# A two-layer hybrid decoder on one core: second layer's weights split in the first layer's pair stage, feed-forward operand without its norm, output projection in two half-K parts

## What is computed

```python
for l in range(DEPTH):
    h = rms_norm(x, norm_gains[l, 0])
    z = h @ w_in[l]
    z_main, z_mem = z[..., :MAIN_W], z[..., MAIN_W:]
    if l < N_A_LAYERS:
        y_main = pool_mixer(z_main, w_pool[l], pool_scale[l])
    else:
        y_main = dilated_mixer(z_main, positions, shared)
    y_mem = memory_attn(z_mem, mem, mem_norm[l], w_mkv[l])
    y = jnp.concatenate([y_main, y_mem], axis=-1) @ w_out[l]
    x = x + rms_norm(y, norm_gains[l, 1])
    h = rms_norm(x, norm_gains[l, 2])
    gu = h @ w_gate_up[l]
    y = (jax.nn.silu(gu[..., :D_FF]) * gu[..., D_FF:]) @ w_down[l]
    x = x + rms_norm(y, norm_gains[l, 3])
    if l == N_A_LAYERS - 1:
        shared = build_shared_kv(x, positions, kv_norm, w_kv)
```

## Time and profile before

| | |
|---|---|
| median of the runs | 2314.24 us (2311.76 to 2314.56) |
| profiled execution | 2309.91 us, of it the span 2308.0 us |
| TensorE busy | 2150.7 us, 93% |
| VectorE busy | 1337.2 us, 58% |
| ScalarE busy | 880.6 us, 38% |
| GpSimd busy | 264.9 us, 11% |
| HBM traffic | 170.04 MB read, 43.12 MB written |
| mean granted TensorE clock | 0.972 of full |

### The profile page before, as it was taken

How to read it: one execution, slowest core, us unless ns; L and a number is a source line. 1 busy time by engine, 2 the same in 40 slices (tenths; PEclk the granted TensorE clock), 3 DMA queues, 4 the chain that set the end, 5 groups by cost and what they waited for, 6 DMA issues and landing times.

```text
span 2308.0 us, 24943 instructions
## 1 busy us (share of the span) xinstructions
PE 2150.7 (93%) x9554; PEld 1719.2 (74%) x9554; DVE 1337.2 (58%) x1984; ACT 880.6 (38%) x1375; POOL 264.9 (11%) x136
## 2 busy tenths in 40 slices
PE   5997999999999999987999999895999999999996
PEld 4775877888888887875777767673788888888785
DVE  7355287566666626456445446469846666662543
ACT  5335343222223425232545556564422222242420
POOL 4442100000000000043122215120000000000000
PEclk9998999999999999998999999997999999999998
DMA  4202051222223536450000000014222222262533
GB/s 155 89 14 94 25 177 50 82 83 82 82 82 120 200 129 211 129 203 18 19 28 28 28 25 12 24 47 146 83 78 82 82 82 82 101 222 90 208 122 107
DMA packets 69382, 214.77 MB, mean 93 GB/s; under 512 B 7825, under 2 KB 10129, under 8 KB 64017
## 3 DMA queue, kind: packets, MB, share of 16 engines
q1 hardware_dynamic: 53136, 183.82, 23.1%
q10 hardware_dynamic: 16128, 29.37, 3.8%
HBM read 170.04 MB, written 43.12 MB: 92 GB/s over the span
## 4 chain that ended last, share of the span: by engine, by line
PE 79%; DVE 12%; issue 3%; ACT 3%; DMA 2%; POOL 0%; ACTq 0%; SPq 0%; DVEq 0%
PE PS L772 10%; PE PS L773 10%; PE PS L774 10%; PE PS L589 8%; PE PS L590 7%; PE PS L592 7%; PE PS L792 7%; PE PS L794 6%; PE PS L793 6%; PE PSC L697 4%; PE PO L671 2%; DVE SS L1436 2%; DVE RSTD L1428 1%; PE PTR L681 1%; DVE PR L1539 1%
## 5 line engine op out<-in xcount | busy, mean ns | idle before, releaser
L792 PE MATMUL PS<-IH,DH 128*128 128x512 f32 x704 | 275.7, 392 | 3.3 <-DVE IL L1744 2.9
L794 PE MATMUL PS<-IH,DL 128*128 128x512 f32 x704 | 274.0, 389 | 0.0
L793 PE MATMUL PS<-IL,DH 128*128 128x512 f32 x704 | 274.0, 389 | 0.0
L772 PE MATMUL PS<-BHT,SH 128*128 128x512 f32 x576 | 224.1, 389 | 0.0
L773 PE MATMUL PS<-BLT,SH 128*128 128x512 f32 x576 | 224.1, 389 | 0.0
L774 PE MATMUL PS<-BHT,SL 128*128 128x512 f32 x576 | 224.1, 389 | 0.0
L589 PE MATMUL PS<-XH,WH 128*128 128x512 f32 x448 | 196.0, 437 | 26.7 <-DVE XL L1566 21.2
L590 PE MATMUL PS<-XL,WH 128*128 128x512 f32 x448 | 180.7, 403 | 0.0
L2073 POOL TENSOR_TENSOR WR<-WR,GN 128x1024 f32<-128x1024 f32 x28 | 59.8, 2140 | 1003.8 <-DMA WR<-in_w 983.6
L2079 POOL TENSOR_TENSOR WL<-WR,WH 128x1024 fp32r<-128x1024 f32 (+2 forms) x66 | 145.3, 2203 | 217.0 <-ACT WH L899 217.0
L772 PE MATMUL PS<-BH,SH 128*128 128x512 f32 x432 | 168.0, 389 | 0.0
(11 more groups left out here) (205 smaller groups left out, 4327.8 us busy)
## 6 DMA issues: line engine op xcount, KB each, us to landing
DR<-in_wdn SPq DMA_DIRECT2D x64, 704.0 KB, 4.1
SR<-in_wst SPq DMA_DIRECT2D x36, 1024.0 KB, 5.2
WR<-in_w SPq DMA_DIRECT2D x60, 512.0 KB, 3.5
IR<-inner SPq DMA_DIRECT2D x88, 256.0 KB, 5.7
inner<-TP SPq DMA_DIRECT2D x36, 512.0 KB, 4.4
TP<-x_mid ACTq DMA_DIRECT2D x48, 256.0 KB, 3.0
x_mid<-YOA ACTq DMA_DIRECT2D x32, 256.0 KB, 2.7
XS<-in_x SPq DMA_DIRECT2D x16, 256.0 KB, 6.3
```

Of the source, the lines that this page charges most:

```text
L772: MM(BANK[bank], SH[b][:, w, c], BH[t][:, k, :], start=(k == 0), stop=False)
L792: MM(bank, wh[:, i, :], IH[r][:, :], start=(k == 0), stop=False)
L793: MM(bank, wh[:, i, :], IL[r][:, :], start=False, stop=False)
L794: ins = MM(bank, wl[:, i, :], IH[r][:, :], start=False, stop=(k == NF - 1))
```

## The change

It has five parts.

**1. Layer 1's weights for "mem", "in" and "kv" (24 blocks, `PRE`) are split during layer 0's pairs.** In sixteen pairs (f = 4 to 19), one and two weights in turn, SyncE loads a weight, ScalarE applies the gain in eight 128-wide copies and makes hi in one 1024-wide copy, GpSimd makes lo, and SyncE stores both to a buffer in HBM. In layer 1 both parts are loaded in place of the raw weight, and neither ScalarE nor GpSimd has work with them.

```diff
+def presplit(o):
+    return o.l == 1 and o.name in ("mem", "in", "kv")
...
+PRE = [n for n, o in enumerate(JOBS) if o.share is None and presplit(o)]
+PRE_AT = {n: i for i, n in enumerate(PRE)}
+NV = 3
+PRE_PAIRS = 16
+def prepared(f):
+    a, b = (len(PRE) * min(max(g - NHT, 0), PRE_PAIRS) // PRE_PAIRS for g in (f, f + 1))
+    return range(a, b)
...
+            def keep_weight(i):
+                b, o = i % NV, JOBS[PRE[i]]
+                act.wait_ge(v_loaded[b], 16 * (i // NV + 1))
+                for k in range(KT):
+                    ins = A(VR[b][:, k, :], VR[b][:, k, :], ACT.Copy, scale=GN[:, 8 * o.gain + k:8 * o.gain + k + 1])
+                    ins.then_inc(v_gained, 1)
+                act.wait_ge(v_gained, KT * (i + 1))
+                A(VH[b][:, :, :], VR[b][:, :, :], ACT.Copy).then_inc(v_hi, 1)
...
-                    silu_first(q)
+                    if l == 0:
+                        silu_first(q)
+                        for i in prepared(f):
+                            keep_weight(i)
                     if f < NF - 1:
...
+            for i in range(len(PRE)):
+                pool.wait_ge(v_hi, i + 1)
+                G_.tensor_tensor(VL[i % NV][:, :, :], VR[i % NV][:, :, :], as_f32(VH[i % NV][:, :, :]),
+                                 ALU.subtract).then_inc(v_lo, 1)
...
+                        for i in prepared(f - 2):
+                            keep_weight(i)
+                        for i in prepared(f):
+                            load_kept(i)
```

```diff
-                pe.wait_ge(ss_done[h], 8 * (s + 1))
-                px_begin(("norm", s, h))
-                MM(PX[:, :], ONES, SS[:, HALF[h]], start=True, stop=True).then_inc(px_full, 1)
-
...
+            def norm_columns(s, h):
+                if s:
+                    pe.wait_ge(ss_done[h], 8 * s)
+                else:
+                    pe.wait_ge(ss0_done, 8)
+                px_begin(("col", s, h))
+                for t in range(4):
+                    c = HT * h + P * t
+                    ins = MM(PX[:, t:t + 1], SS[:, c:c + P], ONE, start=True, stop=True)
+                ins.then_inc(px_full, 1)
+            def norm_rows(s, h):
+                rows.append((s, h))
+                pe.wait_ge(rc_done, len(rows))
+                px_begin(("row", s, h))
+                for t in range(4):
+                    ins = nc.tensor.transpose(PX[:, P * t:P * (t + 1)],
+                                              RC[:, 4 * h + t:4 * h + t + 1].to_broadcast([P, P]), IDENT)
+                ins.then_inc(px_full, 1)
...
+            def norm_row(s, h):
+                px_read(("row", s, h), lambda: A(RSTD[:, HALF[h]], PX[:, :], ACT.Copy))
...
-            def norm(s, h):
-
-                dve.wait_ge(px_free, px_at[("norm", s, h)])
-                V.reciprocal(RSTD[:, HALF[h]], RSTD[:, HALF[h]]).then_inc(rstd_done[h], 1)
+            def invert(s, h):
+                dve.wait_ge(px_free, px_at[("col", s, h)])
+                V.reciprocal(RC[:, 4 * h:4 * h + 4], RC[:, 4 * h:4 * h + 4]).then_inc(rc_done, 1)
```

```diff
+                if r == 3:
+                    A(bh(h, k), YO[h][:, k, :], ACT.Copy, scale=GN[:, 48 + k:49 + k]).then_inc(x_hi[h], 1)
...
+            def scale_x(h, k):
+                act.wait_ge(x_lo[h], 16 + k + 1)
+                act.wait_ge(*x_stored(3, h, k))
+                A(YO[h][:, k, :], YO[h][:, k, :], ACT.Copy, scale=GN[:, 48 + k:49 + k]).then_inc(x_scaled, 1)
...
+                if r != 3:
+                    V.tensor_tensor(y, y, RSTD[:, c], ALU.mult).then_inc(y_normed[h], 1)
                 dve.wait_ge(y_normed[h], 8 * (r - 1) + k + 1)
...
+            def scaled_low(h, k):
...
+                V.scalar_tensor_tensor(out=bl(h, k), in0=YO[h][:, k, :], scalar=GN[:, 48 + k:49 + k],
+                                       in1=as_f32(bh(h, k)), op0=ALU.mult, op1=ALU.subtract).then_inc(x_lo[h], 1)
...
+            def gate_scaled(f, h):
+                j = J[("ffn", 1, (f, 0), h)]
+                dve.wait_ge(mm_done, j + 1)
+                if f == 0:
+                    rstd_seen(6, h)
+                else:
+                    dve.wait_ge(prod_done, 2 * NHT + NHT * h + f)
+                V.tensor_tensor(T[1][:, HALF[h]], BANK[banks(j)[0]], RSTD[:, HALF[h]], ALU.mult).then_inc(gate_out, 1)
...
+            def scale_pair(q):
+                dve.wait_ge(c12_done, q + 1)
+                dve.wait_ge(c11_done, q + 1)
+                V.tensor_tensor(G[:, :], G[:, :], RSTD[:, :], ALU.mult).then_inc(g_scaled, 1)
+                dve.wait_ge(c22_done, q + 1)
+                dve.wait_ge(c21_done, q + 1)
+                link(V.tensor_tensor(UP[:, :], UP[:, :], RSTD[:, :], ALU.mult))
...
+            def y_norm(h):
+                pool.wait_ge(px_free, px_at[("row", 5, h)])
+                for k in range(KT):
+                    G_.tensor_tensor(YO[h][:, k, :], YO[h][:, k, :], RSTD[:, HALF[h]],
+                                     ALU.mult).then_inc(y_normed[h], 1)
+            def st_add(q):
+                b = SR[q % 2]
+                pool.wait_ge(*st_seen(q))
+                link(G_.tensor_tensor(b[:, S1, :], b[:, S3, :], b[:, A22, :], ALU.add))
+                link(G_.tensor_tensor(b[:, S3, :], b[:, A11, :], b[:, S3, :], ALU.subtract))
+                link(G_.tensor_tensor(b[:, S2, :], b[:, S1, :], b[:, A11, :], ALU.subtract))
+                G_.tensor_tensor(b[:, S4, :], b[:, A12, :], b[:, S2, :], ALU.subtract).then_inc(st_added, 1)
```

```diff
-OUT_ORDER = ((3, 4, 5, 0, 1, 2, 6, 7), (6, 7, 0, 2, 4, 1, 3, 5))
+OUT_ORDER = ((3, 4, 5, 0, 1, 2, 6, 7), (6, 0, 2, 4, 1, 3, 5, 7))
...
             for n, o in enumerate(run):
                 o.slot = n % 4
             jobs += run
-            jobs += [Job("out", 1, m, k0=5, kn=3, halves=(h,), tag=h, slot=wide(m),
-                         share=("out", 1, m, 0) if h else None) for h in range(2) for m in range(KT)]
+            for part in range(2):
+                jobs += [Job("out", 1, m, k0=4 * part, kn=4, halves=(h,), tag=(part, h), slot=10 + 8 * part + m,
+                             share=("out", 1, m, (part, 0)) if h else None) for h in range(2) for m in range(KT)]
...
+        def score_bank(a):
+            return BANK[3] if a > TWO_BANKS and a % 2 else BANK[4]
...
-        counts = [7] * 6 + [5, 6, 6] + [5, 5, 6] * 3
+        counts = [5, 5, 6, 0] + [5, 5, 6] * 4 + [5, 6]
...
-        for m in range(4):
-            HOOKS[J[("out", 1, m, "early")]] = (0, 1, 2, 3, 4)
+        for m in range(KT):
+            HOOKS[J[("out", 1, m, (0, 0))]] = (1, 2, 3) if m < 5 else (1, 3)
+            HOOKS[J[("out", 1, m, (0, 1))]] = (0, 1, 2, 3) if m < 2 else (1, 3) if m < 7 else (1,)
...
-                    places = {(0, 2, 0): {7: [("norm", s_x, 1)]}}
+                            job(J[("out", 1, m, (1, h))], ch, cl, ks=OUT_ORDER[1][4:],
+                                wait_k=(lambda k: pe.wait_ge(c_lo, 15 + OUT_ORDER[1].index(k)))
+                                if m == 0 and h == 0 else None,
```

```diff
+            def x0_low(k):
+                dve.wait_ge(x0_hi, k + 1)
+                V.scalar_tensor_tensor(out=XLA[:, :, k, :], in0=XS[:, k, :].rearrange("p (h c) -> p h c", h=2),
+                                       scalar=GN[:, k:k + 1], in1=as_f32(XHA[:, :, k, :]), op0=ALU.mult,
+                                       op1=ALU.subtract).then_inc(x0_lo, 1)
```

888 lines of the change are left out of this document (529 added, 359 removed).

## The result

The changed kernel took 2400.39 us (median of four runs, 2396.6 to 2405.07) beside 2313.89 us for the kernel before: a ratio of 1.0376, interval 1.0355 to 1.0398. It is slower by 3.8%, where 2295 us was forecast, and it lies outside the range (2255 to 2330). All that follows is counted in the profiled execution, 2402.4 us with a span of 2400.4.

The account below looks back on a forecast made before the run. TensorE was 93% busy, so only its idle time, lower clock and new waits could move the time. Terms outside layer 0's pairs summed to -73.8, with +55 there -18.8: 2291.1 us profiled, 2295 as median, range 2255 to 2330.

Parts of the forecast that it names:

- the sum of the gains: All stages except layer 0's pairs: the separate gains and small losses added up to -73.8 us.
- The pairs: Layer 0's pair stage: early weights between silu and first hi make the next pair late, +55 us.
- the 63 of the rows: Layer 0's pairs: sixteen pairs' lateness with GpSimd's collision and the lower clock, 63 us.
- Layer 0's output and feed-forward: Layer 0's output projection and feed-forward: a 4.8 us gap and the clock after it go, -7.5 us.
- Down stages: Both layers' down stages: splits queued behind the cheaper norm come on time, -1.5 us in each.
- Boundary: Between the layers: GpSimd idle, VectorE's additions and subtractions fast again, -22 us (-16 to -25).
- Start: Kernel start: one wide split per tile, squares after, GpSimd held until then, -10.5 us (-5 to -14).
- Attention: Attention: two score banks and steps among output jobs give room, net -17 us (-8 to -24).
- Late output and feed-forward: Layer 1's late output and first feed-forward jobs: no norm before the operand, -15 us (-27 to 0).
- The third rival: Late stage: the unnormalised operand only moves the wait, gaining nothing there; -3.8 in all, 2310 us; chance 0.13.
- Layer 1's pairs: Layer 1's pair stage: ScalarE is free of weights and GpSimd adds the blocks, +1 us.
- The rival "slower": Layer 0's pairs: weights stall them by more than 9.2 us per two pairs, a loss, 2339 us; chance 0.20.

Follow-up runs that it names:

- e2: Changed kernel without the eight 128-wide gain copies of each early weight, the wide hi copy left in place; 2348.26 us, ratio 1.0141.
- s3: Changed kernel without the gain copies for the second weight of each pair that has two; 2383.95 us, ratio 1.0273.
- q1: Kernel before with the early split, its ScalarE work behind the hi of the sums, and the change's new norms; 2287.86 us, ratio 0.9883.
- f3: e1 with inner tiles 20 and 21 given one semaphore each instead of a shared one; 2311.25 us, ratio 0.998.
- p1: Kernel before with the early split alone, placed as in e1, and 14 semaphores for the inner tiles; 2302.28 us, ratio 0.9931.
- h2: e1 with f1, f3, f4 and, in layer 1's first feed-forward jobs, the second half's y norm sums first and weights reordered; 2292.73 us, ratio 0.9898.
- e1: Changed kernel with the early weights' ScalarE work moved behind the hi of the next pair's sums; 2319.24 us, ratio 1.0009.
- e4: Changed kernel with the scores of all attention steps in one bank; 2402.79 us, ratio 1.0377.
- s1: e1 with the logarithm and exponential of each group's second-tile combination replaced by one 128-wide copy; 2314.72 us, ratio 0.9978.
- f1: e1 with y times rstd of layer 1's output moved from GpSimd back to VectorE; 2316.33 us, ratio 0.9997.
- f4: e1 with the last group's combination begun one output job earlier; 2314.19 us, ratio 0.9989.

## Why the prediction was wrong

The step that failed most is the sum of the gains: -73.8 us was forecast outside layer 0's pairs and +15.0 measured, because new waits stood behind the removed ones. By stage, attention missed by 34 us, the late output and feed-forward by 18, the two down stages by 13, the boundary by 9, the start by 8 and the input projection behind it by 5. The pairs missed by 22.

**The pairs: mechanism right, a term of the sum too small.** The weight on ScalarE was taken as 3.3 us and measured 3.44; the lock between GpSimd and VectorE was taken as 0.9 and measured 0.95 (2.70 against 1.75). What was short is the clock: 1.7 us per long gap, from a window of 3.4 us at 0.57; here each gap has a stretch of 6.8 us at half clock, some 5.6 of it behind the gap, and it pushes the next silu from T+9.2 to T+11.9, 2.7 us. Two pairs were forecast 1.5 + 4.7 + 1.7 = 7.9 late and are 9.7 late: 5.2 in the long one (24.28 - 19.04) and 4.5 in the short one, its 1.5 and 3.0 by the clock. Eight times 9.7 are the 77.4. Of the 14.4 us above the 63 of the rows the clock is 10 and the longer chain 4. And the step in which I chose failed: the rows gave 63 with collision and clock, and I took 55. The prediction itself wrote that over 420 us the stall is deeper than the chain that I followed; at 420.8 it is, by the clock's part. The Trainium skill ("SBUF — State Buffer", Who interferes with whom) calls the lock exclusive. The collisions agree: in the kernel after, in e2 and in s3 VectorE's subtraction of 1536 columns lasts 2.70, 3.37 and 3.88 us, and in all three it ends 1.62 us behind GpSimd's. So a collision costs what GpSimd has left of its instruction, and not a fixed 0.9; e2 shows 2.78 us for an addition of 0.69.

**Layer 0's output and feed-forward: right.** Forecast -7.5, measured -7.1 (198.5 to 191.4). The gap of 4.8 us (0.5 now) and its stretch at the lower clock are gone; q1 shows it without the rest of the change (191.3).

**Down stages: -1.5 in layer 0 forecast, +7.8 measured; -1.3 in layer 1 with the end, +2.3 measured.** The first step that failed is the reading of the diff: halving the number of semaphores stood there, and I priced the norm alone. The second and third jobs are 5.0 us longer in layer 0 and 5.4 in layer 1; f3 takes 4.3 and 4.9 back. The second is the term "at most 1 us" for reloading twice the bytes. Layer 0's stage ends with the start of layer 1's first memory matmul, and that waits for the memory's reload from HBM. The row before:

```profile
PE PS L623 <- DMA RSTDM<-rstd_keep: 0.3, 1, 0.3
```

After, it is 3.2 us. From issue to landing the last of these loads took 6.9 us before (997.43 to 1004.33) and 9.7 after (1075.12 to 1084.85), with two loads for each split weight just ahead of it instead of one. In p1, the early split on the kernel before, the wait is 3.2 as well: these are the 3 us that stay in layer 0 in h2, p1 and q1. The norm itself gave 1.3 us in jobs 17 and 18 of each layer, lost 1.3 again in job 29 of layer 0, and made the end 1.8 us shorter (22.2 to 20.4), where 2.5 was forecast.

**Boundary: -22 forecast, -12.8 measured.** It is 48.6 us. The additions are fast again (0.69 us each), but the clock is as low as before (0.83). In place of two waits for the norms' sums, 16.4 us, there is one of 4.7 us for the memory values, which were ready in time before, with 6.8 us at half clock. And the wait of 3.2 us for the reload, just before the stage, is followed in it by 9.4 us at half clock. In e1 the same wait is 2.8 us and no such stretch follows; its stage is 4.0 us shorter. This stretch comes in some kernels and not in others with the same boundary, so the 43.3 of h2 isn't a repair. That "the clock stays low" was my own lower bound, -16, and even that was too good.

**Start: -10.5 forecast, -2.6 measured**, and 4.8 us lost in the stage behind it, for which I had nothing. TensorE still waits 9.4 us for the first split and 7.0 for the sum of squares. The step that failed for the second wait is that putting GpSimd's start behind the splits of x takes the collision away. It moved it on to the sums, which now stand behind the splits (VectorE, then GpSimd, kernel after):

```profile
28.33 3.87 DVE L1605 TENSOR_TENSOR SS<-SS,TP 128x1024 f32<-128x1024 f32 x3
32.57 11.95 DVE L1605 TENSOR_TENSOR SS<-SS,TP 128x1024 f32<-128x1024 f32 x4 [0.36 <-ACT TP L1153]
```

```profile
31.67 2.81 POOL L2347 TENSOR_TENSOR WL<-WR,WH 128x1024 fp32r<-128x1024 f32 x1 [5.41 <-ACT WH L1004]
...
40.56 2.88 POOL L2341 TENSOR_TENSOR WR<-WR,GN 128x1024 f32<-128x1024 f32 x1
```

Three additions, begun while GpSimd is idle, take 1.2 us each, the next four, beside its four instructions, 2.7 to 3.2: 7 us more, as long as TensorE's wait. No run had GpSimd held back further, so what the start would gain by it isn't shown. The start also varies by several us where nothing in it was edited (65.7 before and 71.0 in p1; 62.3 to 65.1 among the kernels with the change's start), so this term is known no better than that.

**Attention: -17 forecast, +16.8 measured** (+5.9, with 10.9 us of matmuls gone to the late part). This is the largest error, 34 us. Four steps of it failed. The steps of attention hooked into the output jobs were taken as a gain. They are the same steps moved: before the output jobs there are 107 at 1.75 us each before, and 91 at 1.77 after (what that stretch takes beyond its 864 matmuls of 512 columns, divided by the steps). The two banks gave 3.6 us (e4), and the wait for the normalised probabilities is no smaller: 9.1 us in 5 times instead of 7.0 in 10. I had no term for ScalarE's copy of the transposed probabilities (PT), which waits its turn among ScalarE's other work. Before and after:

```profile
PE PO L671 <- ACT PT L997: 5.9, 9, 1.2
```

```profile
PE PO L777 <- ACT PT L1111: 14.9, 8, 4.9
```

And the wait for the last combination was taken as 3 to 4 us from "less work behind it"; it is 8.9, since 9.1 us of VectorE and the logarithm and exponential stand in it (s1). From 2.0 us into that gap the clock is at half for 10.2 us, 3.4 of them behind the gap. I had not followed that chain in the trace of before at all.

**Late output and feed-forward: -15 forecast, +2.7 measured** at equal work. The third rival's outcome came: the wait only moved, from the normalised operand to a weight's lo queued behind the second half's residual. Its mechanism, GpSimd's y*rstd against VectorE, was the smaller part: 2.3 us by f1. I had written "the second half's tiles begin behind the first half's sums, gates and weight splits"; that the splits stand behind the tiles too was in the order of the work. h2 shows that 11.5 us were to be had: -9.0 at equal work. The longest wait left there is one of 6.1 us for a norm's sums. The prediction also read the granted clock as near 1 outside the boundary, where the earlier trace rows give 0.91 for this stage: it had no term for the clock here.

**Layer 1's pairs: +1 forecast, +2.8 measured.** Their first 5.7 us are at half clock, behind a wait of 3.1 us for VectorE's multiplication of a gate by rstd (L1841). In p1 and q1, without the change's operand, the stage is as before (342.7); in f1 and f4, where no stretch at half clock comes there, it is 342.8. So the pairs themselves cost nothing more.

**The rival "slower".** Its sign came true. Its point of decision, 9.2 us per two pairs, was passed (9.7), but it isn't the reason: with free pairs (e1) the kernel would have been level, not faster. The point rested on the 73.8 us of gains, and these were absent. The chance of 0.22 for slower was too small because eight gains had been added up with no allowance for several failing together.

**What stays open.** Which of the two remaining parts (half-K output, unnormalised operand) loses how much by itself; no run had one without the other. What the remaining 4.4 us before the late part would give if the combination stood elsewhere. And why the input projection of layer 0 is some 4 to 5 us longer than before (153.0) in all kernels with the change's start (156.6 to 158.3) and not in q1 (154.5): the trace shows where, a wait of 5.9 us instead of 2.0 before the first scores (after and before), for a ScalarE copy behind the hi of a weight whose load came late, and 3.4 us more at half clock; why the load came late isn't shown.

## What to carry to other kernels

Work that fills an idle engine goes behind the last link of a chain that releases TensorE, not between two links: here the same weights cost 77 us in one place and nothing three lines further down. When it runs on two engines, taking part of it away can move the rest into a worse place (e2, s3). A stall that exceeds the slack is paid twice once it is several us long, by the gap and by the stretch at half clock behind it, which also delays the next link. Before a gain is added up, ask of each removed wait which wait stands next behind it, and look in the diff for semaphores and queues that two things now share; a sum of many small gains deserves a wide discount.

## What the runs showed of the hardware

With a gap of TensorE of 4.94 us came 6.8 us at the granted clock of 0.50, beginning 1.1 to 1.3 us before the gap's end; with gaps of 3.9 and 4.0 came 3.4 or 6.8 us; with eight gaps of 2.1 us one stretch of 3.4; behind gaps of 1.5 us it stayed at 1.00. A subtraction on VectorE with two SBUF inputs that began while GpSimd was at work ended 1.62 us behind GpSimd's last instruction, whether it took 2.70, 3.37 or 3.88 us. An addition of 0.69 took 2.78 us when GpSimd began a subtraction of 1024 columns 0.4 us before it, so it waited for nearly the whole of GpSimd's instruction; against a row of 512-wide ones on GpSimd, VectorE's operations went from 0.74 to 1.75 each, the two engines taking turns. The last of three loads from HBM took 9.7 us from issue to landing with two loads for each weight issued ahead of it, and 6.9 with one.
